# Joint root of renorm and norm, skewed attention order, and residual additions between low parts at three stage ends

## The reference

```python
def rms_norm(x, g):
    y = x32 * lax.rsqrt(jnp.mean(x32 * x32, axis=-1, keepdims=True) + EPS)
    return y * g
for i in range(DEPTH_2):
    h = modulate(rms_norm(x, ln_ffn1[i]), sh1, sc1)
    x = x + 0.5 * g1 * swiglu(h, ffn1_wg[i], ffn1_wu[i], ffn1_wd[i])
    ...
    x = rms_norm(x, ln_out[i])
```

## Time and profile before

| | |
|---|---|
| median of 3 runs | 1643.37 us (1642.56 to 1644.06) |
| the profiled execution's own time | 1643.02 us |
| its span, first to last instruction | 1641.2 us |
| TensorE matmul busy | 1584.2 us, 97% |
| VectorE busy | 1100.9 us, 67% |
| ScalarE busy | 740.9 us, 45% |
| mean granted TensorE clock | 0.982 |
| DMA from HBM | 339.17 MB, 208 GB/s over the span |

### The profile page before, as it was taken

How to read it: one execution, slowest core, us unless ns; L and a number is a source line. 1 busy time by engine, 2 the same in 40 slices (tenths; PEclk the granted TensorE clock), 3 DMA queues, 4 the chain that set the end, 5 groups by cost and what they waited for, 6 DMA issues and landing times.

```text
span 1641.2 us, 30633 instructions
## 1 busy us (share of the span) xinstructions
PE 1584.2 (97%) x12598; PEld 1534.9 (94%) x12598; DVE 1100.9 (67%) x1323; ACT 740.9 (45%) x822; POOL 12.9 (1%) x32
## 2 busy tenths in 40 slices
PE   7999999899999989999999899999999999999998
PEld 6999998789999979999987789999899999999998
DVE  5777779867777756777765667777644456754444
ACT  5333354363333654333566553334533345554333
POOL 2000000000000000000000000000000000000000
PEclk8999999799999999999999899999999999999999
DMA  7988753258888438888443278886455554545551
GB/s 230 356 290 281 268 167 129 77 162 298 297 288 279 160 101 297 301 291 283 147 137 126 79 242 288 298 285 229 129 179 179 184 174 155 180 131 183 191 180 59
DMA packets 244678, 341.03 MB, mean 208 GB/s; under 512 B 5891, under 2 KB 188315, under 8 KB 244624
## 3 DMA queue, kind: packets, MB, share of 16 engines
q1 hardware_dynamic: 242656, 334.72, 60.9%
q0 software_dynamic: 1968, 5.54, 1.0%
HBM read 339.17 MB, written 2.63 MB: 208 GB/s over the span
## 4 chain that ended last, share of the span: by engine, by line
PE 87%; DVE 7%; ACT 4%; issue 1%; DMA 1%; SPq 0%; DVEq 0%; ACTq 0%
PE bank L1263 28%; PE bank L1264 27%; PE bank L1265 27%; PE bank L1373 2%; DVE w_lo L775 2%; ACT w_hi L436 2%; DVE arena L970 1%; PE bank L1322 1%; ACT xn L446 1%; DVE xn L915 1%; DVE x_res L932 1%; DMA raw<-in_ffn_w_in 1%; ACT L440 0%; PE bank L1579 0%; DVE xn L803 0%
## 5 line engine op out<-in xcount | busy, mean ns | idle before, releaser
L1263 PE MATMUL bank<-xs_hi,w_hi 128*128 128x256 f32 x2496 | 712.4, 285 | 13.2 <-DVE xs_lo L781 8.7
L1264 PE MATMUL bank<-xs_lo,w_hi 128*128 128x256 f32 x2496 | 707.6, 283 | 0.0
L1265 PE MATMUL bank<-xs_hi,w_lo 128*128 128x256 f32 x2496 | 707.4, 283 | 0.0
L775 DVE TENSOR_TENSOR w_lo<-raw,w_hi 128x2048 fp32r<-128x2048 f32 x245 | 560.3, 2288 | 214.4 <-ACT w_hi L436 206.2
L436 ACT ACTIVATE w_hi<-raw 128x2048 fp32r<-128x2048 f32 x245 | 466.5, 1905 | 232.9 <-PE bank L1265 224.3
L1263 PEld LDWEIGHTS bank<-xs_hi,w_hi 128*128 128x128 f32 x2496 | 480.4, 192 | 22.2 <-issue 21.6
L1264 PEld LDWEIGHTS bank<-xs_lo,w_hi 128*128 128x128 f32 x2496 | 480.5, 192 | 0.7 <-issue 0.7
L1265 PEld LDWEIGHTS bank<-xs_hi,w_lo 128*128 128x128 f32 x2496 | 480.4, 192 | 0.0
L1263 PE MATMUL bank<-gu_hi,w_hi 128*128 128x256 f32 x960 | 274.6, 286 | 0.0
L1265 PE MATMUL bank<-gu_hi,w_lo 128*128 128x256 f32 x960 | 271.7, 283 | 0.0
L1264 PE MATMUL bank<-gu_lo,w_hi 128*128 128x256 f32 x960 | 271.5, 283 | 0.0
(11 more groups left out here) (222 smaller groups left out, 1238.5 us busy)
## 6 DMA issues: line engine op xcount, KB each, us to landing
ada<-in_ada_w SPq DMA_DIRECT2D x72, 1024.0 KB, 5.6
raw<-in_ffn_w_in SPq DMA_DIRECT2D x44, 1024.0 KB, 6.6
raw<-in_ffn_wg SPq DMA_DIRECT2D x44, 1024.0 KB, 5.4
raw<-in_ffn_wu SPq DMA_DIRECT2D x44, 1024.0 KB, 5.3
raw<-in_ffn_wd SPq DMA_DIRECT2D x44, 1024.0 KB, 5.1
raw<-in_ffn_w_out SPq DMA_DIRECT2D x22, 1024.0 KB, 6.5
raw<-in_attn_w_qkv SPq DMA_DIRECT2D x12, 1024.0 KB, 5.1
raw<-in_w_in SPq DMA_DIRECT2D x10, 1024.0 KB, 5.4
```

The costliest lines, as they stand in the source:

```text
L775: dve.tensor_tensor(w_lo[:, s, :], raw[:, s, :], w_hi[:, s, :].bitcast(F32), ALU.subtract)\
L1263: pe.matmul(out_, a_hi, b_hi, start=start, stop=False, skip_group_check=True)
L1264: pe.matmul(out_, a_hi, b_lo, start=False, stop=False, skip_group_check=True)
L1265: return pe.matmul(out_, a_lo, b_hi, start=False, stop=stop, skip_group_check=True)
```

## The change

Four things are done.

Joint root. For stages 5 and 9, which follow a renorm, the norm's mean square is taken of the x from before the renorm, with each tile's squares weighted by the renorm's gain: ScalarE squares x with scale `joint_g`, which is the root of gain squared plus EPS, made once in stage 0. With EPS squared as bias of Ln this gives the product of both roots. The scale of the next norm is then `joint_a`, which has the gain in it. The renorm's own root comes from a second set of squares without scale (`plain_square`), summed into bank MISC after the first set; ScalarE takes it after the rounding of xs, and VectorE writes the renormed x (`renormed`) after the fourth chunk's low part of the next ffn stage. In ple the squares of tiles 0 to 5 are made ahead of the last sigmoid. The constants of a layer (`modulation`) are made at the end of the ffn stage that brings the last of them (stages 2 and 7) instead of ahead of stages 5 and 9. The `FILL` matmuls of stages 4, 5, 8 and 9 go away.

Attention order. The chunks come as Q0 K0 Q1 V0 K1 Q2 V1 K2 Q3 V2 K3 V3. The loop is written out, TensorE's chunks are cut in halves with the small matmuls between them, the logits have two buffers, and the sub-norms of pairs 0 and 1 run within the pairs after them. The output projection uses banks 2, 4, 5 and 0 and starts with heads 0 to 3 while the last two heads are still in work.

Residual additions between low parts. At the end of mix and sgu VectorE makes the low part of the last projection chunk, adds tiles 0 and 1, makes the next low part, adds tiles 2 to 5, makes the third, and adds tiles 6 and 7. At the end of the attention it is low part, tiles 0 to 5, low part, tiles 6 and 7, low part.

The rest is bookkeeping: one more memset, other counts of semaphores, the order of `COLS`.

The diff, cut to its core:

```diff
+JOINT = [n > 0 and STAGES[n - 1][0] == "renorm" for n in range(len(STAGES))]
+SQ_NO = [sum(not j for j in JOINT[:n]) for n in range(len(STAGES))]
...
 for _name, _n in [("ffn1_norm", 8), ("mix_norm", 8), ("ffn2_norm", 8), ("ple_norm", 8), ("final_norm", 8),
-                  ("ln_ffn1_2", 16), ("ln_mix_2", 16), ("ln_ffn2_2", 16), ("ln_out_2", 16),
+                  ("ln_out_2", 16), ("ln_ffn1_2", 16), ("ln_mix_2", 16), ("ln_ffn2_2", 16),
...
+        logit = [carve(2 * SKEW).rearrange("p (c j) -> p c j", c=2) for _ in range(2)]
...
-        SUB_BANK = [3, 2, 3, 3]
+        SUB_BANK = [6, 6, 3, 3]
+        Q_AT, K_AT, V_AT = [0, 2, 5, 8], [1, 4, 7, 10], [3, 6, 9, 11]
+        OUT_BANK = [2, 4, 5, 0]
...
-            pool.wait_ge(memsets, 7)
+            pool.memset(eps_sq[:, :], EPS * EPS).then_inc(memsets, 1)
+            pool.wait_ge(memsets, 8)
...
+            def square(n, k):
+                if n == 0:
+                    act.wait_ge(x_in[k * X_PARTS // KT], 16)
+                else:
+                    act.wait_ge(x_ready, 8 * (n - 1) + k + 1)
+                if n + 1 < len(STAGES) and JOINT[n + 1]:
+                    at = 8 * (n // 8) + k
+                    act.activation(xn[:, k, :], x[:, k, :], ACT.Square, scale=joint_g[:, at:at + 1]).then_inc(sq_ready, 1)
+                else:
+                    act.activation(xn[:, k, :], x[:, k, :], ACT.Square).then_inc(sq_ready, 1)
+
+            def plain_square(k):
+                act.activation(ub[:, k, :], x[:, k, :], ACT.Square).then_inc(ev("plain_sq"), 1)
...
             def norm(n):
                 kind = STAGES[n][0]
-                act.preload_act_table_set(LN_EXP)
-                for k in range(KT):
+                joint = n + 1 < len(STAGES) and JOINT[n + 1]
+                if not JOINT[n]:
+                    act.preload_act_table_set(LN_EXP)
+                    for k in range(6 if n == 4 else 0, KT):
+                        square(n, k)
+                        if joint and k < 6:
+                            plain_square(k)
+                    if joint:
+                        for k in (6, 7):
+                            plain_square(k)
...
+                    act.wait_ge(ss_ready, n + 1)
+
+                    act.activation(rstd[:, 0:T], bank[STAT][:, 0:T], ACT.Ln, bias=(eps_sq if joint else eps_col)[:, :])\
+                        .then_inc(log_ready, 1)
+                    act.wait_ge(log_ready, n + 1)
+                    act.activation(rstd[:, 0:T], rstd[:, 0:T], ACT.Exp, scale=-0.5).then_inc(rstd_ready, 1)
...
+                if JOINT[n]:
+                    act.wait_ge(ss_ready, n + 1)
+                    act.activation(rstd[:, T:2 * T], bank[MISC][:, 0:T], ACT.Ln, bias=eps_col[:, :]).then_inc(log_ready, 1)
+                    act.wait_ge(log_ready, n + 1)
+                    act.activation(rstd[:, T:2 * T], rstd[:, T:2 * T], ACT.Exp, scale=-0.5).then_inc(rstd_ready, 1)
...
+                    at = COLS["final_norm"][0]
+                    act.activation(joint_g[:, :], cols[:, at:at + 2 * KT], ACT.Square).then_inc(ev("joint_sq"), 1)
+                    act.wait_ge(ev("joint_sq"), 1)
+                    act.activation(joint_g[:, :], joint_g[:, :], ACT.Sqrt, bias=eps_col[:, :]).then_inc(ev("joint_g"), 1)
+                    act.wait_ge(ev("joint_g"), 1)
...
+                    if j == 3:
+                        for k in range(6):
+                            square(n + 1, k)
+                            plain_square(k)
...
+                split(c + 2)
+                qk_in(0, 0)
+                split(c + 3)
+                qk_root(0, 0)
+                for i in range(1, 4):
+                    qk_in(i - 1, 1)
+                    split(c + K_AT[i])
+                    if i >= 2:
+                        turned(i - 2, 1)
+                    qk_root(i - 1, 1)
+                    split(c + Q_AT[i] + 3)
+                    qk_in(i, 0)
+                    if i >= 2:
+                        outs(i - 2)
+                        sub_squares(i - 2)
+                    heads(i - 1, 0)
+                    values(i - 1)
+                    qk_root(i, 0)
+                    if i >= 2:
+                        sub_root(i - 2)
+                    turned(i - 1, 0)
+                    heads(i - 1, 1)
+                    split(c + V_AT[i - 1] + 3)
+                    if i >= 2:
+                        highs(i - 2)
+
+                qk_in(3, 1)
+                split(c + 13)
+                turned(2, 1)
+                qk_root(3, 1)
+                values(3)
+                outs(2)
                 split(c + 14)
-                sub_root(0)
+                sub_squares(2)
                 heads(3, 0)
-                sub_root(1)
-                turned(3, 0)
                 heads(3, 1)
                 sub_root(2)
-                highs(range(4))
+                turned(3, 0)
+                highs(2)
                 turned(3, 1)
                 outs(3)
                 sub_squares(3)
...
-                highs(range(6, 8))
+                highs(3)
...
+            def renormed(n, root):
+                scale, _ = norm_cols(n)
+                for k in range(KT):
+                    dve.scalar_tensor_tensor(out=x[:, k, :], in0=x[:, k, :], scalar=scale(k), in1=root,
+                                             op0=ALU.mult, op1=ALU.mult).then_inc(x_ready, 1)
...
-                dve.wait_ge(rstd_ready, n + 1)
+                if n + 1 < len(STAGES) and JOINT[n + 1]:
+                    return
+                dve.wait_ge(rstd_ready, n + 1 - JOINT[n])
                 if STAGES[n][0] == "renorm":
-                    for k in range(KT):
-                        dve.scalar_tensor_tensor(out=x[:, k, :], in0=x[:, k, :], scalar=scale(k), in1=rstd[:, 0:T],
-                                                 op0=ALU.mult, op1=ALU.mult).then_inc(x_ready, 1)
+                    renormed(n, rstd[:, 0:T])
                     return
...
                 split(c0 + 3)
+                if JOINT[n]:
+                    dve.wait_ge(t_ready, 8 * SPLIT_NO[n] + 8)
+                    dve.wait_ge(rstd_ready, n + 1)
+                    renormed(n - 1, rstd[:, T:2 * T])
                 gu_mul(0, c0 + 1)
...
+                if f in (1, 3):
+                    modulation(f // 2)
                 gu_low(STEPS - 1)
...
-            def residual(n, done):
+            def residual(n, done, banks=range(4), ks=range(KT)):
...
 
             def projected(n, c):
 
-                residual(n, lambda b: (chunks_done, c + b + 1))
+                done = lambda b: (chunks_done, c + b + 1)
+                split(c + 3)
+                residual(n, done, ks=range(2))
+                split(c + 4)
+                residual(n, done, ks=range(2, 6))
+                split(c + 5)
+                residual(n, done, ks=range(6, KT))
...
+                at = COLS["final_norm"][0] + 8 * layer
+                link(dve.tensor_tensor(joint_a[:, 8 * layer:8 * layer + 8], a_col[:, layer, 0:8], cols[:, at:at + 8],
+                                       ALU.mult))
...
-                split(c + 13)
-                split(c + 14)
-                split(c + 15)
                 projected(n, c + 10)
...
-                pair(0, False)
-                with dve.Fori(1, 4) as i:
-                    pair(i, True)
+                split(c + 2)
+                split(c + 3)
+                qk_out(0, 0)
+                for i in range(1, 4):
+                    split(c + K_AT[i])
+                    qk_out(i - 1, 1)
+                    split(c + Q_AT[i] + 3)
+                    scored(i - 1, 0)
+                    weights(i - 1, 0)
+                    scored(i - 1, 1)
+                    qk_out(i, 0)
+                    if i >= 2:
+                        sub_norm(i - 2)
+                    weights(i - 1, 1)
+                    split(c + V_AT[i - 1] + 3)
+                    if i >= 2:
+                        lows(i - 2)
+                split(c + 13)
+                qk_out(3, 1)
                 scored(3, 0)
-                sub_norm(0)
+                scored(3, 1)
                 split(c + 14)
                 weights(3, 0)
-                scored(3, 1)
-                sub_norm(1)
                 weights(3, 1)
                 sub_norm(2)
-                lows(range(6))
+                lows(2)
                 sub_norm(3)
-                lows(range(6, 8))
+                lows(3)
                 split(c + 15)
+                residual(n, lambda b: (chunks_done, c + 12 + b + 1), OUT_BANK, range(6))
                 split(c + 16)
+                residual(n, lambda b: (chunks_done, c + 12 + b + 1), OUT_BANK, range(6, KT))
...
             def norm(n, after=False):
                 if n and not after:
                     pe.wait_ge(consts_in, 16)
+                if JOINT[n]:
+                    return
+                joint = n + 1 < len(STAGES) and JOINT[n + 1]
+
+                def plain(ks):
+                    for k in ks:
```

(70 more changed lines are left out.)

258 lines of the change are left out of this document (114 added, 144 removed).

## The result

The changed kernel takes **1616.11 us** (median of 4, 1614.76 to 1618.3) against 1643.71 us (4 runs) for the kernel before: a ratio of 0.9837, 95% interval 0.9824 to 0.985. The forecast was 1617.4 us in a range of 1612 to 1624. The profiled execution of the changed kernel is the slowest of its four, 1618.3 us with a span of 1616.5; the three others had spans of 1613.0 to 1615.1. So the two profiled executions differ by 24.7 us (1641.2 less 1616.5), and the medians by 27.6.

What follows compares the result with a forecast made beforehand. Stages were taken as bound by TensorE, gains lying at seams and in the attention: 9.65 + 5.4 + 12.3 - 1.4 = 26.0 us, the median going from 1643.4 to 1617.4 us, range 1612 to 1624.

Steps and rivals of the forecast that it cites:

- The joint root at stage 5: Seam ahead of stage 5: one root round instead of two brings the first product 9.65 us earlier.
- The rival with two loads: In ple, squares between sigmoids reload the table: 2.6 us lost at stage 5, 1620 us; chance 0.05.
- At stage 9: Seam ahead of stage 9: the joint root brings the first product 5.4 us earlier.
- What moved into stages 5 and 9: Second root and eight renorm operations ahead of the first gate product: hidden, 0.3 us to spare at stage 5.
- The attention: The attention's new order: 126 us instead of 138.3, 12.3 us won, with 6.3 us of waits left.
- a pair takes more than 23 us: Sign that the prediction is wrong: a pair of heads in the attention takes longer than 23 us.
- rival 1: ScalarE's queue becomes the attention's bound: 9 of the 12.3 us gone, 1626 us, half of that 1622; chance 0.10.
- its lower bound: Attention: 6 us won if each pair stays at 24.4 us and only half of the end is won.
- Rival 3: Attention: the overlap at the end doesn't happen, only 4 of 12.3 us won, 1625.7 us; chance 0.04.
- Rival 4: Attention pairs: TensorE falls to 1.2 GHz, 5.76 us per chunk, 1652 us with 6 of 16 chunks; chance 0.03.
- The stage ends: Ends of mix, sgu and attention: new order costs 0.75, 0.65 and zero, 1.4 us lost in all.
- if the ends gain: Sign that the prediction is wrong: the ends of mix, sgu and attention get shorter instead of losing 1.4 us.

Runs made afterwards that it cites:

- e5: The changed kernel with the joint root undone, renorm and norm each taking their own squares, sums and root: 1633.47 us.
- e7: The changed kernel with the eight renorm operations in the fifth and ninth stages made twice, first into a tile nobody reads: 1623.86 us.
- e2: The changed kernel with joint_g's Square, Sqrt and table load moved from the first ffn stage to the third: 1615.17 us.
- e4: The changed kernel with five tiles instead of four in the first part of each attention pair's k chunk, ahead of the transpose: 1616.21 us.
- e10: The changed kernel with e4's edit, an earlier last sub-sum, the low part ahead of all attention residual additions, and no second table load after attention: 1613.17 us.
- e8: The changed kernel with the attention's three projection chunks run whole behind the last sub-sum, not in parts between small matmuls: 1626.57 us.
- e1: The changed kernel with the ends of mix, attention and sgu in the old order, all low parts ahead of the residual additions: 1614.44 us.
- e11: The changed kernel with e9, e10 and e2 together, and the Ln and Exp table loaded earlier at the ends of mix and sgu: 1605.29 us.
- e9: The changed kernel with the last low part of weights made behind the last two residual additions at mix and sgu: 1610.54 us.
- e3: The changed kernel with the 12 squares between ple's last two sigmoids moved behind the last sigmoid and its table load: 1621.89 us.
- e6: The changed kernel with three 128x512 matmuls of constants in each of four TensorE waits, at three stage ends and in attention: 1625.92 us.

## Why the prediction was right, point by point

**The joint root at stage 5** (9.65): 9.89 in the profiles and 10.0 against e5. Its parts held too: the first product 2.65 us after Ln (2.71), the plain sums on time. The two squares of a tile took 0.71 us of ScalarE (584.37 to 585.08), where 0.73 was reckoned. **The unknown**, a square between two sigmoids, took no table load. The rival with two loads falls; the Trainium skill ("ScalarE: Activation LUTs", section "Table sets: the hidden batching unit") leaves square out of the functions that every set holds, and this trace shows that it runs under the sigmoid's table as it does under Ln and Exp's: twelve of them between 584.37 and 588.71, with the next load at 589.21.

**At stage 9** (5.4): 5.66, and 5.6 against e5. The parts held here too: Ln stands 4.07 us after the last product, 0.77 more than before (0.95 forecast), and the first product waits for TensorE's own eight plain sums, which take 3.26 us (3.55 forecast):

```profile
1134.77 3.62 PE L1383 MATMUL bank<-ub,ones_d 128*128 128x256 f32 x16
1138.03 0.47 PE L1322 MATMUL bank<-xs_hi,w_hi 128*128 128x256 f32 x1
```

**What moved into stages 5 and 9** (hidden, 0.3 us to spare at stage 5): hidden, with 0.55 and 0.7 to spare, which e7 showed from the other side. What the forecast priced too low is the loss without cover: not "at most 3.3 each" but the wait plus a spell of 1.7. The constants of stages 2 and 7 made no wait; these stages kept their 198.1 and 198.5 us.

**The attention** (12.3, to 126.0): 126.5, and 125.4 in the executions without a spell. I had allowed up to 1.7 for one behind the wait of 2.3; it cost 1.15. The waits that are left add up to 5.4 us (5.7 in e2) and not 6.3; with e2's the content is 119.7, against the 120 of the forecast. One sign of being wrong came true, "a pair takes more than 23 us": a pair takes 24.7. The fault is in the sign. The forecast's own terms, 17.3 of chunks, 6 of small work, a sub-sum of 0.9 and a wait of 0.8, give a pair of 25, and its sum of 120 + 6.3 rests on these and not on the 22 that rival 1 and the sign assume. So the premise of its lower bound came true (each pair stays at 24.4), but the end was won whole and not by half. The old low clock, too, was read too simply: it fell first from 900.0 to 903.4, and in the 12 us ahead of 910 TensorE was busy for 6.35, so it had waited for about half of them and not for most. Rival 1 (ScalarE the bound) falls by e4 and e10: moving TensorE's work took the waits away without another one. Rival 3 falls by e8, which builds what that rival describes, and costs 8.9 us, not the 8.3 that it was priced at. Rival 4 (the clock falls in the pairs) didn't come.

**The stage ends** (1.4 lost, "the part that I expect to lose"): the order itself loses 0.55 at mix and 0.49 at sgu and wins 0.3 at the attention, 0.74 in all. The mechanism was the named one (VectorE waits 2.29 us for squares, and the low part stands ahead of the last additions), the term twice its true size. The forecast's last sign of being wrong, "if the ends gain", holds for the attention alone, where the forecast had zero. It came close to a false alarm at sgu: by the profiles alone attention and sgu did gain, 0.55 and 0.75, and only e1 shows what the old order takes beside the other parts of the change and without a spell: 7.35 at sgu, not 8.59, so that the new order's 7.84 is a loss of 0.49 there, and 7.08 at the attention, not 7.34. e1's own medians would not have shown it: 1.7 us is within the scatter.

**The sum** (26.0) met 24.7 in the profiles, since the start, put at nothing, took 2.1 us more in that execution; without it the other terms make 26.8 to 27, near the 27.6 of the medians. The start is no term of the change by e2, e8 and e11, but a profile is one draw: four executions of one kernel differ by 3.5 us, and the stretches at 1.2 GHz, which differ from run to run, are where the traces show that much. Taken from executions without a spell after the change, the terms are 10.0, 5.6, 13.0 (138.40 less 125.39) and -0.74, which is 27.9 us: each a little better than forecast, so the sum didn't come out by errors that cancel.

What the forecast missed is not in its sum but beside it: it found that the low part at the end of mix "was made in the time in which VectorE now waits", and did not ask where VectorE waits after the change. It waits for the root, 3.43 us at mix (with a spell) and 2.22 at sgu, and e9 put the low part there.

## What to carry to other kernels

- When a long operation of one engine must be placed near a serial chain of reductions, put it behind the last operation that the chain needs, into the engine's own wait for the result, and not between parts of what it needs.
- Squares and other inputs of a norm belong into the idle time of their engine ahead of the last input, even where this delays that input a little: here over 4 of 10 us came from it.
- Price a new wait of over 2 us in a dense stage at more than its length, and compare seams only between executions without a low clock in them; with medians scattered by 2 us, effects of 0.5 us are read from seams, not from times.

## What the runs showed of the hardware that was not expected

- **A spell at 1.2 GHz doesn't follow a given wait each time.** The wait of 2.4 us at the end of mix stands in nine profiled executions (after, e2 to e8, e10); in four of them (after, e3, e4, e5) the clock was 0.50 for the next 3.4 us, in five it stayed. In the four that lack the wait (before, e1, e9, e11) it never fell there. By the Trainium skill ("TensorE: Matmul & The Clock Gate", section "What's actually happening") the clock is held up by activity; the trace agrees as far as that goes, each of these falls coming behind a wait of 2.4 us; what decides between the two outcomes of one wait, no run here shows.
- **The same lengths to 0.02 us.** Stages and seams without a spell agree between kernels that share their order there (7.50, 7.50, 7.51, 7.51 at mix; 7.24 in eight kernels at the fifth stage). Between the profiled executions nearly all scatter is thus in the start and in the clock; of the other executions there is no trace.
- **A square with a pointer scale** costs 0.09 us more than a plain one (0.50 against 0.41), and in the alternating row the pair takes 0.71, where 0.73 was reckoned.
- **A 128x512 matmul of plain fp32** shows as two rows and takes 0.86 us (six rows in 2.58), though the profile gives 0.59 as the length of one row: such a matmul is priced by the starts, not by a row. Three times 0.59 is the 1.8 us that was expected of e6's fill.
